# Two-layer mixer trunk: the last TensorE turns go to the DMA, and the vector engine's order around them is rewritten

## The reference

```python
x = x + 0.5 * swiglu_ffn(rmsnorm(x, norm_ffn1[l]), w_ffn1_in[l], w_ffn1_out[l])
u = rmsnorm(x, norm_mix[l]);  proj = u @ w_in[l]
q, k, v, g, p, c, gates = jnp.split(proj, split_points, axis=-1)
y_ret = (retention(q, k, v, positions) * jax.nn.silu(g)) @ w_ret_out[l]
y_pool = pool_mixer(p, w_pool[l], pool_scale[l])
# conv_module: u = a * sigmoid(b); y = causal depthwise conv of 31 taps + conv_b;
#              y = silu(layernorm(y)); return y @ w_conv_out
y_conv = conv_module(c, conv_w[l], conv_b[l], conv_ln_g[l], conv_ln_b[l], w_conv_out[l])
merged = gates[:, :, 0] * y_ret + gates[:, :, 1] * y_pool + gates[:, :, 2] * y_conv
x = x + merged @ w_out[l]
x = x + 0.5 * swiglu_ffn(rmsnorm(x, norm_ffn2[l]), w_ffn2_in[l], w_ffn2_out[l])
```

## Time and profile before

| | |
|---|---|
| time, median of 3 runs | 1125.2 us (1124.42 to 1127.37) |
| time of the profiled execution | 1124.31 us |
| its span, first to last instruction | 1122.5 us |
| TensorE busy | 1115.9 us, 99% |
| VectorE busy | 802.8 us, 72% |
| ScalarE busy | 654.6 us, 58% |
| GpSimd busy | 37.7 us, 3% |
| granted TensorE clock, mean | 0.999 of full |

### The profile page before, as it was taken

How to read it: one execution, slowest core, us unless ns; L and a number is a source line. 1 busy time by engine, 2 the same in 40 slices (tenths; PEclk the granted TensorE clock), 3 DMA queues, 4 the chain that set the end, 5 groups by cost and what they waited for, 6 DMA issues and landing times.

```text
span 1122.5 us, 13054 instructions
## 1 busy us (share of the span) xinstructions
PE 1115.9 (99%) x4997; PEld 923.7 (82%) x4997; DVE 802.8 (72%) x992; ACT 654.6 (58%) x750; POOL 37.7 (3%) x67
## 2 busy tenths in 40 slices
PE   9999999999999999999999999999999999999998
PEld 7888888888888888888888888888888888888886
DVE  6856566899999875655476655378999987665553
ACT  6765446664658765554475554376637577656441
POOL 0100000000200000000000000000002001000000
PEclk9999999999999999999999999999999999999999
DMA  9985665773866786666497666467738667866551
GB/s 367 313 277 197 228 236 180 255 215 125 258 223 194 211 284 216 206 204 225 143 309 240 210 201 228 170 218 249 199 122 281 234 197 231 267 215 225 159 187 38
DMA packets 131822, 245.18 MB, mean 218 GB/s; under 512 B 101024, under 2 KB 101408, under 8 KB 107184
## 3 DMA queue, kind: packets, MB, share of 16 engines
q1 hardware_dynamic: 129408, 237.53, 63.7%
q0 software_dynamic: 1648, 6.06, 1.4%
q10 hardware_dynamic: 704, 0.75, 0.2%
HBM read 219.16 MB, written 1.05 MB: 196 GB/s over the span
## 4 chain that ended last, share of the span: by engine, by line
PE 97%; ACT 1%; DMA 1%; DVE 1%; issue 0%; POOL 0%; POOLq 0%; ACTq 0%; DVEq 0%
PE acc L434 31%; PE acc L435 31%; PE acc L436 31%; PE acc L478 1%; PE acc L483 1%; PE acc L487 1%; DMA retT_planes<-ret_planes 1%; PE ret L701 0%; ACT w_hi L840 0%; PE tr L621 0%; ACT v L1089 0%; ACT ret_planes L1081 0%; ACT pin L1072 0%; PE tr L613 0%; PE ret L633 0%
## 5 line engine op out<-in xcount | busy, mean ns | idle before, releaser
L1290 DVE TENSOR_TENSOR w_lo<-raw,w_hi 128x2048 fp32r<-128x2048 f32 (+2 forms) x204 | 445.6, 2213 | 85.4 <-ACT w_hi L840 85.3
L840 ACT CAST w_hi<-raw 128x2048 fp32r<-128x2048 f32 (+2 forms) x204 | 375.4, 1849 | 215.6 <-PE acc L436 202.4
L434 PE MATMUL acc<-w_hi,xT_hi 128*128 128x512 f32 x1152 | 450.6, 391 | 0.0
L436 PE MATMUL acc<-w_hi,xT_lo 128*128 128x512 f32 x1152 | 448.5, 389 | 0.0
L435 PE MATMUL acc<-w_lo,xT_hi 128*128 128x512 f32 x1152 | 448.2, 389 | 0.0
L436 PEld LDWEIGHTS acc<-w_hi,xT_lo 128*128 128x128 f32 x1152 | 216.2, 188 | 45.2
L434 PEld LDWEIGHTS acc<-w_hi,xT_hi 128*128 128x128 f32 x1152 | 216.3, 188 | 44.9 <-DVE gates L1599 0.4
L435 PEld LDWEIGHTS acc<-w_lo,xT_hi 128*128 128x128 f32 x1152 | 216.3, 188 | 44.1
L1373 DVE SCALAR_TENSOR_TENSOR h<-acc,rs,silu_gate 128x256 f32<-128x256 f32 x88 | 42.5, 483 | 152.1 <-ACT silu_gate L907 152.1
L434 PE MATMUL acc<-w_hi,hT_hi 128*128 128x512 f32 x348 | 135.4, 389 | 0.0
L435 PE MATMUL acc<-w_lo,hT_hi 128*128 128x512 f32 x348 | 135.4, 389 | 0.0
(11 more groups left out here) (150 smaller groups left out, 657.5 us busy)
## 6 DMA issues: line engine op xcount, KB each, us to landing
raw<-in_weights SPq DMA_DIRECT2D x192, 1024.0 KB, 5.2
raw<-in_weights SPq DMA_DIRECT2D x8, 512.0 KB, 3.5
raw<-in_weights SPq DMA_DIRECT2D x12, 256.0 KB, 7.6
bias<-in_gate_bias POOLq DMA_DIRECT2D x6, 512.0 KB, 6.9
first<-in_first SPq DMA_DIRECT2D x7, 384.0 KB, 5.9
x<-in_x SPq DMA_DIRECT2D x2, 512.0 KB, 12.3
scale_row<-in_pool_scale POOLq DMA_DIRECT2D x2, 512.0 KB, 7.1
hT_planes<-h_planes SPq DMA_TRANSPOSE x54, 3.1
```

The source lines that it names most:

```text
L434: nc.tensor.matmul(o, a_hi, b_hi, start=first, stop=False)
L436: return nc.tensor.matmul(o, a_lo, b_hi, start=False, stop=last)
L840: nc.scalar.copy(w_hi[:, hf % HIGHS, 0:n], raw[:, hf % RAWS, 0:n]).then_inc(hi_split, 1)
L1290: nc.vector.tensor_tensor(w_lo[:, hf % RAWS, 0:n], raw[:, hf % RAWS, 0:n], w_hi[:, hf % HIGHS, 0:n].bitcast(F32), ALU.subtract).then_inc(l ...
```

## The change

All eight columns of `y` blocks and all four merged pieces are turned by the DMA. The identity matrix, its load and `transpose4` are gone. In detail:

- The convolution's sums are turned in two pairs of channel groups (`split_y`, `turn_y`, `y_out`, pair 0 where the front was, pair 1 new). Both land in `y_tokens`, so the layer norm's statistics are one instruction per token tile over 512 numbers, and `ln_apply` is one instruction per tile.
- The last nine taps, before in lots of five and four behind two and four retention merges, stand in one lot behind the first merge. The last retention merge stands behind the layer norm's statistics.
- The layer norm's shift is made on GpSimd (one small multiplication more) from a negated mean that VectorE makes (`ln_negate`).
- Merged piece (0, 0) takes the way of the others: `split_merged`, DMA, `merged_join`, `merged_high`, `merged_low`. TensorE's first matmul of `M_OUT` waits for its `merged_lo_ready`.
- Piece (0, 0) and (0, 1) are both joined and cut before the last merge, `merge(l, CONV, 1, 1)`, which moves behind two subtractions of weights.

```diff
-                in_block(l, M_GATE_CONV, 1, mid={4: lambda: turn_y_back(l)})
...
+                in_block(l, M_GATE_CONV, 1)
...
-                wide(l, M_CONV, M_CONV, 1, side, range(4), True, True,
-                     {(0, 1): lambda: turn_merged(l)})
-                wait_tr_taken(pe, ("m", l))
+                wide(l, M_CONV, M_CONV, 1, side, range(4), True, True)
+                pe.wait_ge(merged_lo_ready, moved(l, 0, 0) + 1)
...
+            def turn_y(l, pair):
+                at = 2 * l + pair
+                sp.wait_ge(y_split, (at + 1) * T)
...
+                    turn_merged(hf // HALVES, 0, 0)
...
+                if hf % HALVES == 2 * M_RET + RAWS:
+                    turn_y(l, 1)
...
                 cast(ahead(M_GATE_CONV))
+                split_y(l, 1, 0)
+                split_y(l, 1, 1)
+                y_out(l, 1)
                 cast(ahead(M_GATE_CONV) + 1)
-                cast(ahead(M_GATE_CONV + 1))
                 ln_apply(l, 0)
                 split_yn(l, 0)
                 ln_apply(l, 1)
                 split_yn(l, 1)
-                gate_tanh(l, CONV, 0, 0)
-                gate_tanh(l, CONV, 0, 1)
-
+                cast(ahead(M_GATE_CONV + 1))
                 conv_silu(l, 0)
                 conv_high(l, 0)
+                gate_tanh(l, CONV, 0, 0)
                 conv_silu(l, 1)
                 conv_high(l, 1)
+                gate_tanh(l, CONV, 0, 1)
                 gate_tanh(l, CONV, 1, 0)
                 cast(ahead(M_GATE_CONV + 1) + 1)
+                split_merged(l, 0, 0)
                 gate_tanh(l, CONV, 1, 1)
                 cast(ahead(M_CONV))
+                split_merged(l, 0, 1)
                 merged_high(l, 0, 0)
-                split_merged(l, 0, 1)
                 split_merged(l, 1, 0)
+                merged_high(l, 0, 1)
                 cast(ahead(M_CONV) + 1)
-                merged_high(l, 0, 1)
                 split_merged(l, 1, 1)
                 cast(ahead(M_OUT))
                 merged_high(l, 1, 0)
...
                 gate_z(l, RET, 1, 1)
-                subs(M_RET)
+                sub(l * HALVES + 2 * M_RET + 3)
                 merge(l, RET, 0, 0, merged_ret)
+                conv_taps(l, CH * TAPS)
+                merge(l, RET, 1, 0, merged_ret)
+                sub(l * HALVES + 2 * M_RET + 4)
+                sub(l * HALVES + 2 * M_GATE_CONV + 3)
                 merge(l, RET, 0, 1, merged_ret)
-                conv_taps(l, 5)
-
-                merge(l, RET, 1, 0, merged_ret)
-                merge(l, RET, 1, 1, merged_ret)
-                conv_taps(l, CH * TAPS)
-                sub(l * HALVES + 2 * M_GATE_CONV + 3)
-                for t in range(T):
-                    ln_stat_front(l, t)
                 for t in range(T):
                     ln_stat(l, t)
                     ln_mean(l, t)
                 ln_eps(l)
+                ln_negate(l)
                 gate_z(l, CONV, 0, 0)
-                ln_shifts(l)
-
                 gate_z(l, CONV, 0, 1)
+
                 sub(l * HALVES + 2 * M_GATE_CONV + 4)
+                merge(l, RET, 1, 1, merged_ret)
+                gate_z(l, CONV, 1, 0)
+                yn_join(l, 0)
                 sub(l * HALVES + 2 * (M_GATE_CONV + 1) + 3)
-                yn_join(l, 0)
-                gate_z(l, CONV, 1, 0)
                 yn_join(l, 1)
                 conv_low(l, 0)
                 sub(l * HALVES + 2 * (M_GATE_CONV + 1) + 4)
...
+                merged_join(l, 0, 0)
                 merged_low(l, 0, 0)
                 merge(l, CONV, 1, 0, merged_all)
+                merged_join(l, 0, 1)
                 sub(l * HALVES + 2 * M_CONV + 4)
+                merged_low(l, 0, 1)
+
+                sub(l * HALVES + 2 * M_OUT + 3)
                 merge(l, CONV, 1, 1, merged_all)
-                merged_join(l, 0, 1)
-                merged_low(l, 0, 1)
-
-                sub(l * HALVES + 2 * M_OUT + 3)
                 merged_join(l, 1, 0)
                 merged_join(l, 1, 1)
                 merged_low(l, 1, 0)
...
+                pool.wait_ge(ln_minus_ready, l + 1)
+                pool.wait_ge(ln_rstd_ready, l + 1)
+                nc.gpsimd.tensor_tensor(ln_shift, ln_minus, ln_rstd, ALU.mult
+                                        ).then_inc(ln_shift_ready, 1)
```

More of the change, by code:

```diff
@@ L108, with trunk @@
 ADDS_BEFORE = {0: CHUNKS - 1, 1: MIX - 1, 3: FFN2 - 1}
-def trunk(nc, x_in, positions, weights_in, gate_bias, pool_scale, norm_final, params, ident_in,
-          inv_freq_in, decay_in, band_in, first_in, out):
+def trunk(nc, x_in, positions, weights_in, gate_bias, pool_scale, norm_final, params, inv_freq_in,
+          decay_in, band_in, first_in, out):
     with ExitStack() as ctx:
@@ L149, in trunk @@
         head_rs = sb("head_rs", [P, T, HEADS])
-        ln_stats = sb("ln_stats", [P, T, 2, 6])
+        ln_stats = sb("ln_stats", [P, T, 6])
         ln_mean_var = sb("ln_mean_var", [P, T, 2])
-        ln_small = sb("ln_small", [P, 3, T])
-        ln_var, ln_rstd, ln_shift = (ln_small[:, i, :] for i in range(3))
+        ln_small = sb("ln_small", [P, 4, T])
+        ln_var, ln_rstd, ln_shift, ln_minus = (ln_small[:, i, :] for i in range(4))
         arena_from = nc.sbuf_base
@@ L348, in moved @@
         def moved(l, t, c):
-            return 3 * l + 2 * t + c - 1
+            return 4 * l + 2 * t + c
         def tokens(t):
@@ L523, in wide @@
                             mid[n, i]()
-            def transpose4(name, sources):
-                wait_tr_free(name)
-                for i, s in enumerate(sources):
-                    mm = nc.tensor.transpose(bank(name)[:, i * P:(i + 1) * P], s, ident)
-                mm.then_inc(tr_full, 1)
-            def turn_merged(l):
-                pe.wait_ge(merged_all, l * 4 + 1)
-                transpose4(("m", l), [merged[:, 0, 0, i * P:(i + 1) * P] for i in range(4)])
-            def turn_y_back(l):
-                if l == 0:
-                    pe.wait_ge(ident_landed, 16)
-                pe.wait_ge(conv_step, (l + 1) * CH * TAPS)
-                transpose4(("y", l), [y[:, c, tokens(t)] for t in range(T) for c in (2, 3)])
             def hT(k, t):
```

105 lines of the change are left out of this document (42 added, 63 removed).

## The result

The change made the kernel slower: 1131.05 us median (1130.40 to 1131.86, 6 runs) against 1125.03 (1124.42 to 1127.37, 6 runs), ratio 1.0052, 95% interval 1.0041 to 1.0063. The forecast was 1129.4 in a range of 1126.6 to 1131.4, slower with 0.66. The profiled execution took 1130.4 us, its span 1128.6.

What follows compares the result with a forecast made beforehand. TensorE, busy 1115.9 of 1122.5 us, was taken as the bound. Two layers x 2.1 = +4.2 us on the profiled 1124.31 gave 1128.5, plus 0.9 to the median, 1129.4; own range 1128.6 to 1130.6, wide range 1126.6 to 1131.4.

Steps and rivals of the forecast that it cites:

- slow turn of y: Rival: second turn of y takes 5.4 us, `M_CONV` begins 0.8 us late in each layer; +5.8, 1131.0 us; chance 0.09.
- Transposes and the convolution product: Up to `M_CONV`: four transpose groups vanish, 0.49 us each; the 0.30 us wait and its 0.12 restart go.
- The 1.55 us a layer that the sum gives back: TensorE, 325.30 to 381.25 us: ten blocks take 55.95 us where 54.40 would do; the excess is all recoverable.
- From there to the second tile: `M_CONV` to second tile's `M_OUT`: late merge chain makes TensorE wait 3.0 us, 3.1 with restart.
- The small wait for a subtraction: Last half of `M_OUT`, first tile: subtraction ends at 364.85, due 364.75; TensorE waits 0.2 us.
- The last merge as the cause: Merge (1,1) completes only at 366.25, so low part (1,0) comes at 371.8, due 368.8.
- The seam: Behind the mixer: sums into x come 3.0 us later; less a 0.9 margin, TensorE ends 2.1 us late a layer.
- the foreseen wait in FFN2's second block: FFN2 begins near 382.8; its second block waits about half a us for `w_lo`.
- The clock: Rival: the 3 us wait drops TensorE to 1.2 GHz, 2.0 us more in each layer, 1133.4 us; chance 0.03.
- The second layer: Counted like the first layer, 2.1 us longer: two layers x 2.1 = +4.2 us.

Runs made afterwards that it cites:

- the early merge: Changed kernel with the last merge, CONV (1,1), moved right behind merge CONV (1,0), ahead of the two subtractions of weights: 1125.36 us.
- the stall taken away: Changed kernel with the low part of piece (1,0) ahead of the join of (1,1), and its high part ahead of ScalarE's cast: 1130.70 us.
- the filler: Changed kernel with ten idle-time matmuls (`keep_busy`) ahead of TensorE's wait at the second tile's output product: 1130.48 us.
- the merged part alone: Kernel before with only the merged pieces handled as in the changed kernel; y, taps and retention merges as before: 1132.45 us.

## Why the prediction was right, and where its sizes were off

The direction, the place and the mechanism held; the size was 1.65 us short (1129.4 against 1131.05). The measured time is above the forecast's own range (to 1130.6) and 0.35 us inside the wide one, whose upper end stood there for a slow turn of y that did not come about. That the time, 1131.05, is the 1131.0 of that rival is chance.

- *Transposes and the convolution product.* Right. The blocks are 5.44 us apart. The first low part began at 346.17 and was done at 346.86, predicted 346.7. The stages that stood at guesses came out so: statistics over 512 numbers 0.69 us (0.7), apply 0.82 (0.6), the added multiplication 0.19 (0.2).

```profile
334.47 0.69 DVE L1609 BATCH_NORM_STATS2 ln_stats<-g_silu 128x6 f32<-128x512 f32 x1
...
339.35 0.81 ACT L1058 ACTIVATE pin<-g_silu,ln_small 128x512 f32<-128x512 f32 x1
...
337.31 0.19 POOL L1878 TENSOR_TENSOR ln_small<-ln_small 128x2 f32<-128x2 f32 x1
```

  These answer to the earlier trace rows. The 1.55 us a layer that the sum gives back measured 1.45 in the first layer, 1.4 in the second (TensorE's lead at 355 and 911 us with the early merge).
- *From there to the second tile.* Right, within 0.2 us at each step. The small wait for a subtraction 0.17 (0.2), the last merge complete at 366.41 (366.25), the first matmul of the second tile at 371.97 (371.8). The transpose of (1,1) landed 3.1 us behind its issue (367.52 to the join at 370.60), the median of the earlier trace rows.
- *The last merge as the cause.* Shown by moving that one line in either kernel: 5.7 us off the changed one, 4.2 onto the one before.
- *The seam.* Right that it, not the stall, sets the end: with the stall taken away the time stayed (1130.70). The sum into x at 372.65, predicted 372.5. In the second layer the seam added 0.73 us, predicted 0.55. In the first it added none and the foreseen wait in FFN2's second block was missing, since the slow matmuls had made TensorE late already (FFN2 began at 384.6, predicted 382.8); with the filler, at full clock, that wait was there (0.23 us at 392.33).
- *The clock.* In the first layer this is the term that was mis-sized. The rival had 0.03 and counted 2.0 us in each layer. The row against it, full clock through 1116 to 1120 with 0.94 us of work, was read one window too short: the last matmul of that trace ended at 1116.9, and its clock did fall, only later (windows of the kernel before):

```profile
1121.00:1122.50 1.50, 0.00 (x0) 0.00 (x0) 0.00 (x0) 0.00 (x0) 0.00 (x0) 0.57 0.40 150
```

  In the changed kernel the clock fell behind the first layer's wait, some 1.4 us after TensorE had gone on; with the merged part alone, in both layers. The slow matmuls cost 1.6 us; with the seam's margin counted in, the first layer was 3.1 us longer instead of 2.1. In six runs the mean clock was 0.996 to 0.999, so it did not fall alike in all of them. For the median the clock explains less than for the profiled run: with filler matmuls and the clock at 1.00 the median was lower by 0.57 of the 1.65 us, and that is not clear of noise. The Trainium skill, "TensorE: Matmul & The Clock Gate", Part 1, has idleness return the array to half rate; the first layer agrees (1.2 GHz behind a wait of 2.59 us), the second does not show it (1.00 behind 2.60). I had thought that the wait would have to grow for this, and it fell at a wait shorter than the 3.0 us forecast.
- *The second layer* is 2.7 longer instead of 2.1, with the clock at 1.00: the transposing DMA of the normalized y took 3.6 us there instead of 3.1 (a load had 2.6 us to go at its issue, 2.1 in the first layer), VectorE's join waited 0.35 us for it, and `M_CONV` and `M_OUT` each began with a wait of 0.1 and a restart of 0.1. The prediction had worked out the first layer only and doubled it. The rival "slow turn of y" named a late landing too, though of another turn, and at a far higher price (5.8 us).

Why the clock fell in one layer and not in the other, behind waits of 2.59 and 2.60 us, stays open. So does the scatter of the runs of the slow versions (2.5 to 3 us, against 1 us for those without long waits).

## What to carry to other kernels

Taking work off the bounding engine pays only if the engines that feed it get no longer in turn: here 1.45 us freed on TensorE were lost because one merge of 1.3 us had moved behind two subtractions of 2.2. When reordering, follow the piece with the longest way still to go (split, DMA of 3.1 us, join, low part: some 5.6 us) and put its start ahead of work that has only its own length. Removing a stall proves little: ask whether the next stage was waiting for the same late result, and look in the profile for idle gaps ahead of the saturated stretch that part of the work could fill.
